# A bidirectional encoder block: three y tiles first in the mix, earlier residual loads, and a reordered start of the first block

## The reference

```python
h = rmsnorm(x, mix_norm_w); proj = h @ w_in            # q k v g (4 heads of 128), a b (512 each)
y_ret  = silu(g) * (groupnorm(retention(rotary(q), rotary(k), v)) * gn_w + gn_b)   # both directions
u      = a * sigmoid(b)
y_conv = silu(layernorm(depthwise_conv31(u) + conv_b) * ln_w + ln_b)
x = x + concat([y_ret, y_conv]) @ w_out                # "the mix"
x = x + cross_attention(rmsnorm(x), rmsnorm(mem))      # 4 heads, 256 memory tokens
x = x + square(relu(rmsnorm(x) @ w_ff1)) @ w_ff2
out = rmsnorm(x)
```

## Time and profile before

| | |
|---|---|
| median of 3 runs | 2901.76 us (2901.56 to 2907.09) |
| the profiled execution | 2901.58 us, its span 2899.8 us |
| PE busy | 2792.1 us, 96% of the span |
| DVE, ACT, POOL busy | 48%, 20%, 31% |
| mean granted TensorE clock | 0.990 |

### The profile page before, as it was taken

The page is one execution under the profiler, slowest core; times in us unless marked ns, Lnnn a source line. Parts: engine busy times, 40 slices in busy tenths (PEclk is TensorE's granted clock), DMA queues, the critical chain, the costliest instruction groups (busy, mean ns, idle before and its releaser), DMA issues.

```text
span 2899.8 us, 36996 instructions
## 1 busy us (share of the span) xinstructions
PE 2792.1 (96%) x13882; PEld 2349.9 (81%) x13882; DVE 1378.6 (48%) x1527; ACT 581.4 (20%) x1062; POOL 885.3 (31%) x439
## 2 busy tenths in 40 slices
PE   7999999998889999999999999999999999999998
PEld 6778888887767998888888888778988888888887
DVE  5875849396864334523315134443336234151343
ACT  6221212122552222100001001232221000010012
POOL 1523334246942000333333333210003233332331
PEclk9999999998999999999999999999999999999999
DMA  4241423338733222111111113132221111111111
GB/s 161 77 164 62 145 91 113 122 105 294 234 133 116 88 88 87 44 47 47 51 43 51 47 47 108 51 131 88 88 80 44 51 46 48 51 43 51 47 48 73
DMA packets 289771, 254.00 MB, mean 88 GB/s; under 512 B 8032, under 2 KB 253976, under 8 KB 283416
## 3 DMA queue, kind: packets, MB, share of 16 engines
q1 hardware_dynamic: 266336, 203.45, 22.6%
q10 hardware_dynamic: 23352, 49.39, 4.7%
HBM read 196.71 MB, written 56.10 MB: 87 GB/s over the span
## 4 chain that ended last, share of the span: by engine, by line
PE 82%; DVE 10%; DMA 2%; issue 2%; ACT 2%; POOL 2%; ACTq 0%; DVEq 0%; SPq 0%; POOLq 0%
PE ps L740 24%; PE ps L735 23%; PE ps L736 23%; DVE acc L1778 5%; PE ps L1107 2%; PE ps L1108 2%; PE ps L1109 2%; POOL wlo L591 1%; PE ps L761 1%; DVE st_f L1868 1%; DMA wb<-wqk_d 1%; DVE alo L1922 1%; PE ps L1069 1%; DVE alo L2054 1%; PE ps L1118 0%
## 5 line engine op out<-in xcount | busy, mean ns | idle before, releaser
L589 POOL TENSOR_SCALAR whi<-wraw 128x1024 fp32r<-128x1024 f32 x192 | 227.7, 1186 | 1887.3 <-PE ps L740 1189.3
L735 PE MATMUL ps<-ahi,whi 128*128 128x512 f32 x1376 | 542.6, 394 | 17.8 <-DVE alo L2054 11.5
L736 PE MATMUL ps<-alo,whi 128*128 128x512 f32 x1376 | 538.0, 391 | 0.0
L591 POOL TENSOR_TENSOR wlo<-wraw,whi 128x1024 fp32r<-128x1024 f32 x192 | 525.8, 2739 | 16.0
L735 PE MATMUL ps<-bhi,whi 128*128 128x512 f32 x1024 | 399.4, 390 | 2.3 <-DVE blo L1975 2.3
L736 PE MATMUL ps<-blo,whi 128*128 128x512 f32 x1024 | 398.4, 389 | 0.0
L1778 DVE SCALAR_TENSOR_TENSOR acc<-upad,taps,acc 128x2048 f32<-128x2048 f32 x120 | 346.0, 2883 | 12.7 <-DVE acc L1775 0.5
L740 PE MATMUL ps<-ahi,wlo 128*128 128x512 f32 x1376 | 340.1, 389 | 0.0
L735 PEld LDWEIGHTS ps<-ahi,whi 128*128 128x128 f32 x1376 | 259.7, 189 | 78.5 <-DVE alo L2054 14.9
L1613 ACT ACTIVATE ahi<-z 128x512 f32 x128 | 80.9, 632 | 1141.0 <-DVE z L2051 1141.0
L735 PE MATMUL ps<-xhi,whi 128*128 128x512 f32 x768 | 303.8, 396 | 3.3 <-ACT st L1321 1.2
(11 more groups left out here) (258 smaller groups left out, 3635.8 us busy)
## 6 DMA issues: line engine op xcount, KB each, us to landing
wraw<-in_w_ff SPq DMA_DIRECT2D x128, 512.0 KB, 3.7
proj_d<-st ACTq DMA_DIRECT2D x64, 256.0 KB, 2.4
wraw<-in_w_in SPq DMA_DIRECT2D x24, 512.0 KB, 4.1
xt<-in_x SPq DMA_DIRECT2D x16, 512.0 KB, 6.1
wraw<-in_w_xkv SPq DMA_DIRECT2D x16, 512.0 KB, 5.0
vwo_d<-pst ACTq DMA_DIRECT2D x16, 512.0 KB, 3.6
wqk_d<-pst ACTq DMA_DIRECT2D x16, 512.0 KB, 3.6
wraw<-in_w_out SPq DMA_DIRECT2D x16, 512.0 KB, 4.7
```

Of the source, the lines that this page charges most:

```text
L589: pool.tensor_scalar(whi[:, slot, :, :], wraw[:, slot, :, :], 1.0, 0.0, ALU.mult, ALU.add).then_inc(w_hi, 1)
L591: pool.tensor_tensor(wlo[:, slot, :, :], wraw[:, slot, :, :], whi[:, slot, :, :], ALU.subtract).then_inc(w_ready, 1)
L735: nc.tensor.matmul(o, whi[:, slot, k, :], hi(k), start=(k == order[0]), stop=False)
L736: nc.tensor.matmul(o, whi[:, slot, k, :], lo(k), start=False, stop=False)
```

## The change

1. **Mix.** SP asks for y tiles 0, 1 and 4 in the iteration of head 2, before it waits for head 2's y, and for the others after it; the weights of blocks 2 and 3 and the first two residual loads are issued there too, ahead of the conv store of the last head. POOL splits the first two weight blocks after it gated head 2, not before. PE starts the mix with tiles 0, 1, 2 in three banks, before the variances of the last conv chunk and before `turn_back`; these variances use bank 7, and their squares 2 and 3 the buffer `w1`. The residual is turned between the banks of the first mix. The barrier is gone, and ACT's conv gates of the last head stand after three of the first four residual steps.
2. **First block.** DVE's decay chain and ACT's Exp and Ln stand before the memory tiles, and so does the load of the positions; the sigmoid and the gating of chunk 3 follow the memory tiles at once. POOL's `wlo` of the first weight block waits until x is scaled (`x_sc` of 4).
3. `rows`, `rstd`, `sq`, `ssq` and `z` change places in memory.

```diff
+        VAR_BANK = (3,) * (HEADS - 1) + (7,)
+        def squares_of(h, c):
+            return w1[:, c - 2, :] if h + 1 == HEADS and c >= 2 else cv_w[:, c % 2, :]
...
 # SP, in the loop over heads
+                if h + 2 == HEADS:
+                    sp.wait_ge(q_rot, HEADS)
+                    sp.wait_ge(y_st, 16 * 2)
+                    sp.wait_ge(c_st, 16 * 2)
+                    for k in (0, 1, 4):
+                        first_y(k)
                 if h + 1 == HEADS:
-                    sp.wait_ge(q_rot, HEADS)
                     sp.wait_ge(y_st, 16 * (HEADS - 1))
-                    for k in Y_ORDER[:KT - 1]:
...
+                    first_y(2)
+                    sp.wait_ge(s_mm, 4 * HEADS)
+                    first_y(5)
+                    first_y(6)
+                    for s in range(2):
+                        load_weights(J_HALF0 + 2 + s, s, w_out[0, :, (2 + s) * P:(3 + s) * P])
+                    sp.wait_ge(c_st, 16 * 3)
+                    for s in range(2):
+                        load_residual(0, s, s)
+                    sp.wait_ge(y_mm, 4 * HEADS)
+                    first_y(7)
                 sp.wait_ge(y_out, 4 * (h + 1))
...
 # POOL, first block and loop over heads
-            proj_split(0, "b", None)
+            proj_split(0, "b", None, scaled=4)
...
-                elif h + 2 == HEADS:
+                if h + 1 == HEADS:
                     for s in range(2):
                         split_weights(J_HALF0 + s, 16 * FILLS * HEADS + 16, s, G_HALF0)
...
 # PE, after the last retained product
-            conv_vars(HEADS - 1)
-            turn_back(HEADS - 1)
...
+                early, rest, late = Y_ORDER[:3], Y_ORDER[3:KT - 1], Y_ORDER[KT - 1:]
...
+                for s, n in S_FIRST[:3]:
...
+                    part(s, n, early, True, False, s == n == 0)
+                turn_back(HEADS - 1)
+                bank_ready(G_HALF0 + 3)
+                pe.wait_ge(c_cen, CT * HEADS)
+                part(1, 1, early, True, False, False)
+                part(0, 0, rest, False, False, True)
+                pe.wait_ge(y_aff, 4 * HEADS)
+                conv_vars(HEADS - 1)
+                part(0, 1, rest, False, False, False)
+                for n in range(NH):
+                    part(0, n, late, False, True, n == 0)
+                for n in range(NH):
+                    turn_residual(0, 0, n, 0)
+                part(1, 0, rest + late, False, True, False)
+                turn_residual(0, 1, 0, 0)
+                part(1, 1, rest + late, False, True, False)
+                pe.wait_ge(c_mul, CT * HEADS)
+                turn_residual(0, 1, 1, 0)
...
 # ACT, first block
-            high_mem()
+            positions_in(0)
             act.wait_ge(dec_dve, 1)
             act.activation(lg[:, 1], lg[:, 0], ACT.Exp, scale=-1.0).then_inc(dec_act, 1)
             act.wait_ge(dec_dve, 2)
             act.activation(lg[:, 3], lg[:, 2], ACT.Ln).then_inc(dec_act, 1)
+            high_mem()
+            gate(0, 3)
...
 # ACT, last head
             y_squares(h, 0)
-            split_high(0, [0, 1, 2])
+            split_high(0, [0, 1])
             y_squares(h, 1)
+            split_high(0, [2])
             y_squares(h, 2)
...
 # DVE, last head
                 if last:
-                    split_low(0, [0, 1, 2])
+                    conv_centre(h)
+                    split_low(0, [0, 1])
+                    square_sums(h, 1)
+                    split_low(0, [2])
```

More of the change, by code:

```diff
@@ L1006, in _, with part @@
                     turn_back(h)
-            conv_vars(HEADS - 1)
-            turn_back(HEADS - 1)
             def first_mix():
-                first, late = Y_ORDER[:KT - 1], Y_ORDER[KT - 1]
-                hi, lo = (lambda k, n: ahi[:, k, n, :]), (lambda k, n: alo[:, k, n, :])
-                for s, n in S_FIRST:
+                early, rest, late = Y_ORDER[:3], Y_ORDER[3:KT - 1], Y_ORDER[KT - 1:]
+                def part(s, n, tiles, begin, end, wait):
+                    o = ps[:, 2 * s + n, :]
+                    for k in tiles:
+                        if wait:
+                            pe.wait_ge(ysp_lo, Y_ORDER.index(k) + 1)
+                        nc.tensor.matmul(o, whi[:, s, k, :], ahi[:, k, n, :], start=(begin and k == tiles[0]), stop=False)
+                        nc.tensor.matmul(o, whi[:, s, k, :], alo[:, k, n, :], start=False, stop=False)
+                    for k in tiles:
+                        last = nc.tensor.matmul(o, wlo[:, s, k, :], ahi[:, k, n, :], start=False, stop=(end and k == tiles[-1]))
+                    if end:
+                        last.then_inc(mm_done, 1)
@@ L1561, in _, with residual @@
                 Q = Q_PER_HALF * h
-                def residual(i, u, hb, qb, norm, order=S_FIRST, half=None):
-                    for idx, (s, n) in enumerate(order):
+                def residual(i, u, hb, qb, norm, order=S_FIRST, half=None, which=range(4)):
+                    for idx in which:
+                        s, n = order[idx]
                         e = 4 * i + idx
@@ L1965, in _, with residual @@
                 Q = Q_PER_HALF * h
-                def residual(i, g, hb, qb, norm, order=S_FIRST, half=None):
-                    for idx, (s, n) in enumerate(order):
+                def residual(i, g, hb, qb, norm, order=S_FIRST, half=None, which=range(4)):
+                    for idx in which:
+                        s, n = order[idx]
                         e = 4 * i + idx
@@ L1995, in _ @@
                     first_sums(0)
-                with dve.Fori(h, KT // 2) as i:
+                    conv_recip(HEADS - 1)
+                    conv_norm(HEADS - 1)
+                    residual(0, G, H, Q, V_XN, half=0)
+                    dve.wait_ge(y_st, 16 * HEADS)
+                with dve.Fori(1, KT // 2) as i:
                     residual(i, G, H, Q, V_XN, half=h)
```

151 lines of the change are left out of this document (69 added, 82 removed).

## The result

The changed kernel took 2882.74 us (median of 4 runs, 2880.0 to 2885.7) against 2902.65 for the kernel before in the same session (4 runs): ratio 0.993, interval 0.9918 to 0.9943, so 16.5 to 23.8 us. The measured time lies within the forecast's range, 2872 to 2889; the forecast itself, 2879.4, is 3.3 us too low. The profiled execution took 2881.92 us with a span of 2880.1, 19.7 less than before.

What follows compares the result with a forecast made beforehand. PE was taken as the bound, busy 96% of the span, so only its waits could be won. From 2901.6 us, 16.3 for the mix and 5.9 for the first block gave 2879.4 us, range 2872 to 2889.

Steps and rivals of the forecast that it cites:

- Part A: Mix: hole 8.78, variances 2.64, first unit 1.37, residual load 2.93, clock behind it 1.62, less 1.0 of new wait: 16.3 us.
- the residual stop and its clock: Mix: PE's 2.93 us stop on a residual load goes, and the slower unit behind it, 1.62 us.
- Step (2): Mix: y tile 2 lands at 834.7, ACT takes it near 836.6; margin 2 us at ACT, 1 at PE.
- Step (3): Mix: GpSimd's moved weight splits run 820.4 to 827.4, are needed at 841.5, and cost DVE nothing.
- late-tile rival: Start of the mix: tile 2 comes late as transfers stack up, PE stands some 4.5 us, 2883.9 us; chance 0.11.
- Step (4): Mix: y's normalising is done by 847.6, when PE comes to it; no wait.
- Step (5): Mix: tiles 5, 6, 7 and head 3's affine; GpSimd's gates meet DVE's splits, PE waits 1.0 us (0.5 to 1.5).
- Part B: First block: PE's start 1.9 us sooner plus the conv taps 4.0 sooner, 5.9 us in all.
- The taps' own 4.0: First block: DVE's shorter path and one fewer meeting with GpSimd's splits start the taps 4.0 us sooner (3.1 to 5.0).
- Blocks 1 to 3 carry 5.9 on unchanged: Later blocks start from PE's own work, so the first block's 5.9 us gain reaches the end whole.
- rival "better": Shorter stops avoid half clock over 105 to 200 us, up to 3 us, mix gains 17.5: 2875.2 us; chance 0.07.
- slow clock of a PE without holes: Mix, 841 to 956 us: PE without holes is granted the low clock, up to 2949 us; chance 0.03.

Runs made afterwards that it cites:

- res_behind: Kernel before with the mix edits alone, residual loads for blocks 2 and 3 and following weights moved behind the last conv store; 2899.0 us, 0.9987 to 1.0006.
- split_late: Changed kernel with GpSimd's two weight splits back in front of the gate of head 2; 2881.2 us, ratio to before 0.9924 to 0.9951.
- no_hold: Changed kernel without GpSimd's wait on the scaling of x in the first block; 2884.3 us, ratio to before 0.9932 to 0.9960.
- masks_behind: Changed kernel with DVE's ten mask instructions moved from ahead of the taps to behind block 0's fourth low half; 2879.8 us, 0.9907 to 0.9936.
- only_mix: Kernel before with the edits of the mix alone, first block as before; 2885.6 us, ratio to before 0.9937 to 0.9964.
- low_early: Changed kernel with DVE's low halves in block 0 behind 12, 14, 18 and 28 taps, not 16, 18, 21 and 31; 2872.2 us, 0.9890 to 0.9921.
- low_all: Changed kernel with low halves behind 12, 14, 18, 28 taps in all four blocks, head 3's last affines ahead of tile 3's split; 2875.7 us, 0.9894 to 0.9922.
- both_late: Mix edits alone, with weight splits ahead of head 2's gate and loads of y tiles 0, 1, 4 behind head 2's store; 2893.3 us, 0.9961 to 0.9983.

## Why the prediction came out as it did

**Part A, 16.3 forecast, 16.1 measured** (52.67 - 36.57). The mechanism held, with the one wait that was named.
- The sum held, its terms did not stand for themselves. I listed the hole (8.78), the unit (1.37), the residual stop and its clock (2.93 + 1.62) as if each went by itself. res_behind shows that the last one undone costs 15.04, not 4.55, with ACT's gates where they now are. No run undoes PE's own order alone, or brings back only the barrier, so their shares stay open.
- Step (2) called tile 2 the thinnest margin. It came when forecast (ACT at 832.68, 836.6 less the 4.0 that all is sooner), and as the step has it, ACT was held there by the squares, not by the load: split_late asks for the tile 7 us later and loses 0.4. The late-tile rival needs both edits undone; its 4.5 us are then 6.2.
- Step (3), splits where they cost nothing: held. Step (4): no wait, held.
- Step (5), a wait of 1.0 (0.5 to 1.5) on y's affine: 1.45, at that place, by that chain. The gate pair took 4.03 instead of 3.22.
- The variances give 6.43 - 3.70 = 2.73, where 2.64 was forecast.

**Part B, 5.9 forecast; 4.0 in the pair of traces, 1.9 on average.**
- PE's start: 1.9 forecast; 1.9 at 80 us and 2.3 at the end of stretch 1 measured (no_hold).
- The taps' own 4.0 (3.1 to 5.0): 5.08 - 2.8 = 2.3 in the pair, where 2.8 is what all of block 0 was sooner; outside my bounds. The start of the chain and the gating behind it came as forecast (2.7 and 0.6, where 2.5 and 0.6 stood). The step that failed is the length of the mask chain: 8.3 us before, about 7.4 in my sum, 9.3 measured. I said that the masks, started earlier, meet one split fewer. They meet two, as before, and lose more in them.
- "Blocks 1 to 3 carry 5.9 on unchanged" failed: 1.7 us go in stretch 2. Stops of 0.2 to 0.9 us in block 2 stand in all four traces with the changed first block and in two of the five with that of before, which is a small part of it. The rest is not settled. Between 660 and 720 us those four spent some 17 us at 1.2 GHz, the five 10 to 17, 13 on average. The 4 us between them would be up to 2 us of work, the size of the loss, but masks_behind has 10 us there and still 387.85, and what decides it was not found.
- My reading rested on one execution. In it GpSimd's first weight block came 0.74 us later than in only_mix (11.02, 10.28), so that more of its split fell beside DVE's scaling: 4.72 against 4.14 us. My range had no term for it.
- The gain named in the rival "better", the clock behind the stops, is real, 3.3 us, but only where the stops go altogether (low_early).

The slow clock of a PE without holes did not come: the clock is full from 706 us to 1842.

So the forecast was right through part A, which is most of it. Part B came at a third of its size on average, and a sum of 22.2 us hides that: the stretches give 16.1 + 1.9 = 18.0, the times 16.5 to 23.8. The range, as stated, is also about 2 us wider on either side than the terms that it names add up to (2874.1 to 2886.9); the result lies within both.

## What to carry to other kernels

When a hole is closed by reordering the engine that waits, list every transfer that is asked for behind a fixed event in that stretch: the earliest of them caps the gain, and the terms do not add (res_behind, low_all). Where an engine waits on a long chain of another, move the handover forward within the chain before shortening the chain: that gave 10.3 us here, and moving ten instructions behind the handover gave 0.8, in part because another engine waited for them there. Judge a gain of 2 us by stretches between events over several traces, not by one pair.

## What the runs showed of the hardware

DVE and GpSimd hold each other for about the rest of an instruction, and reproducibly. A 128x128 scalar_tensor_tensor takes 0.35 us alone and 2.51 to 2.53 in all eight traces with this order in which GpSimd's subtract (2.40 us) had started 0.04 us earlier. One-input tensor_scalars are held as well: 0.96 against 0.29 us at 128x128, 2.50 against 0.43 at 128x512 (89.30 above). The Trainium skill, "SBUF — State Buffer", section "Who interferes with whom", gives both: two SBUF inputs on DVE exclude a GpSimd read of SBUF, and tensor_scalar can run in a mode that takes the shared ports. The traces agree with both, as far as they can show it: they have the durations, not the ports. My prediction used this rule for the gate pair and left it out where it cost most, at the masks.

The low clock has a price beyond its place. PE idled 7.0 us in three stops, and 6.6 us at 1.2 GHz came with them; in both_late 5.0 us of stops brought 0.72 over 12 us.
